# Moving expert additions in the last quarter of the picks from TensorE to VectorE, and moving picks out of one normalisation gap

## The reference

```
ue = jnp.take(u_tab, idx, axis=0)
ve = jnp.take(v_tab, idx, axis=0)
act = jax.nn.gelu(jnp.einsum('thkd,td->thk', ue, t, preferred_element_type=jnp.float32),
                  approximate=False)
return jnp.einsum('thk,thkd->td', (g * act).astype(t.dtype), ve)
```

## Time and profile before

| | us |
|---|---|
| median of 3 runs | 3024.56 (3024.44 to 3024.97) |
| the profiled execution | 3023.42 |
| its span, first to last instruction | 3021.6 |
| TensorE busy | 2738.6 (91%) |
| VectorE busy | 2105.9 (70%) |
| ScalarE busy | 1253.6 (41%) |
| GpSimd busy | 622.1 (21%) |

### The profile page before, as it was taken

The page is one execution under the profiler, slowest core; times in us unless marked ns, Lnnn a source line. Parts: engine busy times, 40 slices in busy tenths (PEclk is TensorE's granted clock), DMA queues, the critical chain, the costliest instruction groups (busy, mean ns, idle before and its releaser), DMA issues. The chain is left out here.

```text
span 3021.6 us, 41715 instructions
## 1 busy us (share of the span) xinstructions
PE 2738.6 (91%) x14564; PEld 2067.9 (68%) x14564; DVE 2105.9 (70%) x4582; ACT 1253.6 (41%) x2946; POOL 622.1 (21%) x531
## 2 busy tenths in 40 slices
PE   6999998889988888798997999599999999999998
PEld 6777788444444444455565777366888989988998
DVE  6895556888878887656687566965546576675887
ACT  3333325444434434555353222354543443333544
POOL 0000000444444444442233233331000000010000
PEclk9999999999999999999998999799999999999999
DMA  6541124999999999999899999995432445543554
GB/s 240 183 168 54 56 91 141 419 420 420 421 417 420 420 419 412 381 418 408 320 399 398 362 417 417 386 376 224 168 133 94 139 149 185 184 149 107 154 184 138
DMA packets 157705, 830.23 MB, mean 275 GB/s; under 512 B 16704, under 2 KB 22080, under 8 KB 91840
## 3 DMA queue, kind: packets, MB, share of 16 engines
q0 software_dynamic: 73728, 536.90, 43.3%
q1 hardware_dynamic: 78240, 271.85, 26.1%
q10 hardware_dynamic: 5536, 18.88, 1.7%
HBM read 825.47 MB, written 2.10 MB: 274 GB/s over the span
## 5 line engine op out<-in xcount | busy, mean ns | idle before, releaser
L750 POOL DMA_INDIRECT slots<-in_experts,consts x295 | 354.2, 1201 | 1036.5 <-DVE consts L2467 521.3
L2492 DVE SCALAR_TENSOR_TENSOR slots<-slots,work 128x1024 f32<-128x1024 f32 x295 | 361.4, 1225 | 93.5 <-DMA slots<-in_experts,consts 81.5
L2091 DVE TENSOR_TENSOR wlo<-w,whi 128x1024 fp32r<-128x1024 f32 x259 | 314.5, 1221 | 70.9 <-ACT whi L1506 70.0
L1078 PE MATMUL psum<-slots,acc 128*128 128x512 f32 x636 | 302.2, 615 | 54.9 <-ACT acc L1724 53.0
L1506 ACT ACTIVATE whi<-w 128x1024 fp32r<-128x1024 f32 x259 | 272.4, 1054 | 138.5 <-PE psum L798 133.4
L750 POOL DMA_INDIRECT split_slots<-in_experts,consts x164 | 200.4, 1222 | 327.6 <-issue 121.6
L1078 PEld LDWEIGHTS psum<-slots,acc 128*128 128x128 f32 x636 | 118.2, 193 | 212.8 <-issue 122.9
L783 PE MATMUL psum<-xres,w 128*128 128x256 f32 x1040 | 240.0, 387 | 0.0
L1712 ACT ACTIVATE consts<-consts 128x1 f32<-128x1 f32 x512 | 100.8, 197 | 333.9 <-DVE slots L2492 190.8
L783 PEld LDWEIGHTS psum<-xres,w 128*128 128x128 f32 x1040 | 198.4, 194 | 46.6 <-issue 20.3
L2492 DVE SCALAR_TENSOR_TENSOR split_slots<-split_slots,work 128x1024 f32<-128x1024 f32 x164 | 200.7, 1224 | 35.8 <-DMA split_slots<-in_experts,consts 29.6
(11 more groups left out here) (367 smaller groups left out, 6030.1 us busy)
## 6 DMA issues: line engine op xcount, KB each, us to landing
w<-in_stream SPq DMA_DIRECT2D x424, 512.0 KB
back_w<-in_back SPq DMA_DIRECT2D x64, 512.0 KB, 3.7
arena<-in_wmod SPq DMA_DIRECT2D x4, 2048.0 KB, 17.2
arena<-in_wmod ACTq DMA_DIRECT2D x8, 1024.0 KB, 5.7
acc<-in_wmod ACTq DMA_DIRECT2D x8, 1024.0 KB, 6.7
slots<-in_experts,consts POOLq DMA_INDIRECT x295
split_slots<-in_experts,consts POOLq DMA_INDIRECT x164
xres<-in_xT SPq DMA_DIRECT2D x1, 2048.0 KB, 9.8
```

The source lines that it names most:

```text
L750: pool.indirect_dma_start(out=slots[slot], out_offset=None, in_=a["experts"], in_offset=bass.IndirectOffsetOnAxis(ap=indices[:, p:p + 1], ...
L1078: mm = pe.matmul(bank(6 + half), diag(p), v[:, half * T:(half + 1) * T], start=(c == 0), stop=(c == PICKS - 1))
L2091: dve.tensor_tensor(wlo[:, s, :, :].rearrange("p k n -> p (k n)"), w32[:, s, :], whi[:, s, :, :].rearrange("p k n -> p (k n)").bitcast(F32 ...
L2492: dve.scalar_tensor_tensor(u, u, 1.0, tokens[:, p // PICKS, :], ALU.mult, ALU.mult, accum_out=inner[:, c:c + 1]).then_inc(sem("dotted"), 1)
```

## The change

Two numbers of the plan are changed. The gap at the end of mlp0 (tile 210) gets the weight 3 and not 8. And `on_dve` also holds from pick 482 on: the picks 482, 483, 486, 487, 490, 491, 494, 495, 498, 499, 502, 503, 506 and 507, seven pairs, are added by VectorE.

```
-    gaps = {SECTIONS["lout0"][0] + 7: 3.5, SECTIONS["pool0"][0] + 1: 3.5, SECTIONS["mlp0"][0] + 63: 8,
+    gaps = {SECTIONS["lout0"][0] + 7: 3.5, SECTIONS["pool0"][0] + 1: 3.5, SECTIONS["mlp0"][0] + 63: 3,
             SECTIONS["xo0"][0] + 7: 3.5, last - 1: LAST_GAP}
...
 def on_dve(p):
 
-    return 336 <= p < 462 and p // 2 % 2 == 1 and p % PICKS < PICKS - 4
+    return (336 <= p < 462 or 482 <= p) and p // 2 % 2 == 1 and p % PICKS < PICKS - 4
```

## The result

The changed kernel is slower: 3039.28 us, median of 5 runs (3035.00 to 3041.82), against 3024.56 us. The ratio is 1.0049, with a 95% interval of 1.0038 to 1.0060. Timed again later, in 12 runs beside 17 of before, it was 3035.34 against 3024.24, ratio 1.0034 (1.0024 to 1.0045). One of these 12 took 6270.86 us, in a slow state; the ratio leaves it out, and the median of the other eleven is 3034.84. Forecast was 3013.4, with a range of 3004 to 3026.

The account below looks back on a forecast made before the run. TensorE was taken to bound the tiles, VectorE the gap behind mlp0, the norm's VectorE-ScalarE chain the smaller gaps. Terms summed to -11.2 us: profiled 3023.42 to 3012.2, median 3013.4, range 3004 to 3026.

Parts of the forecast that it names:

- mlp0: Tiles of mlp0, where TensorE is full: one pair more costs +1.9 us (0.5 to 1.9).
- xq0: Stage behind lout0's gap: no term of its own; the pair that left it was counted in lout0's gap.
- core0: Stage core0: one pair more, between 0 and 1.9 us, half taken, +1.0 us.
- lout0's gap: Gap at lout0's norm: its only pair waits for a late weight and delays the group and scores, +4.1 us.
- xo0: End of xo0: one more pair in the last tile, +0.2; gap without a pair, -8.5; together -8.3 us.
- Rival D: Emptied gap of xo0: whole group at the slow clock, term -4.6 not -8.5; total 3017.3 us; chance 0.12.
- rival B: Transfers set mlp0's pace: terms of xo0, mlp0 and its gap come to nothing; 3031.0 us; chance 0.08.
- The gap of mlp0: Gap behind mlp0, VectorE its chain: six dots and three additions fewer, -11.2 us.
- pool0's gap: Gap at pool0's norm: its pair is weighed later, starts later and delays the group, +5.2 us.
- xo1: Stage xo1: three pairs fewer for TensorE, seven additions more for VectorE, -3.4 us (-5.6 to 0).
- the end: Last picks: one pair fewer, but two additions between VectorE's last dots delay the last one, +3.2 us (0 to 4.5).
- xq1: Rest of xq1: two pairs fewer for TensorE, five additions mostly hidden on VectorE, -3.7 us (-5 to 0).

Follow-up runs that it names:

- the second kernel: The kernel before with only the additions from pick 482 on moved to VectorE, the gap keeping its ten picks: 3022.43 us, ratio 0.9996.
- the eighth: The kernel before with the additions on VectorE from 482 to 503 only, 506 and 507 staying with TensorE: 3017.16 us, ratio 0.9974.
- the second profile: The changed kernel run and profiled once more, nothing altered: median 3035.34 us.

## Why the prediction was wrong

The step that failed most is mlp0's, the overlap of more gathers with full DMA engines, which was put at nothing beside a pair's +1.9; next to it stands xq0, which had no term. By the prediction's own steps:

*core0* (+1.0): the two profiles show +2.3 and +2.4, but kernels with the same plan up to there lie between -1.7 and +2.4. Nothing can be said of it.

*lout0's gap* (+4.1): right in its mechanism to the tenth, 8.45 us of waiting against 8.47, and small by 1.3 to 2.3 us. The term took ScalarE's fourth block from before, 6.7 us behind the column sums; now it comes at 8.5 us (1505.62 to 1514.08), since VectorE scales and adds two rows (0.75 and 1.28 us) ahead of its blocks. From that block to the pair it is 4.17 us, as forecast.

*xq0* (no term): wrong, +3.1. I counted the pairs of the stage and found one fewer. I did not look where in the stage they now stood: the pair that used to follow the second tile follows the first, ahead of the weights that ScalarE makes behind the softmax. In a stage where ScalarE weighs behind something else, a pair costs by its place.

*xo0* (-8.3): the gap itself is right, -7.7 to -7.9 for -8.5. The tiles ahead of it were given 0.2 and cost 2.4, in part since the last residual waits for VectorE, which is at a dot (it starts 1.20 us behind its tile, and 0.03 before), and 5.1 where the clock fell. Rival D, the whole group at the slow clock after the emptied gap, came about for 12 of 32 records: the group takes 8.69 and 1.13 us, with the waits 10.2 from start to end, against 14.2. These slow records cost next to nothing in the changed kernel, since the last four records had to wait 0.39 us for the last block all the same. The Trainium skill's advice against idle gaps (in "TensorE: Matmul & The Clock Gate", "Why this matters for your kernels") was no reason against this edit. The clock was low behind the emptied gap, but it had fallen ahead of it, at about 1624.3 among the norm's sums and products, and it rose 4.9 us into the group. Where a low clock cost time, at the end of xo0, TensorE's waits were of 1.01, 0.32, 0.69 and 1.09 us.

*mlp0* (+1.9): this is the largest mistake, 8.7. It is rival B in part: 6.5 us of it are gone with half the weights' bytes, 2.3 stay, near the forecast. B had a chance of 0.08, and was put aside since VectorE waited only 0.5 us ahead of 42 dots. The sign that the prediction itself gave for B, over 3 us of waits for DMA in mlp0, is there with 12.6. The row says that the gathers were in time, not by how much; the share of 1.02 at 416 GB/s said that nothing could be made up for, and the prediction itself had put the demand at 12.6 us for five more picks. The slack had to be measured, from a transfer's last packet to its dot, and set against that number: it is smallest with 4.5 us at pick 452, and of these some 3 us pass even where a dot waits for nothing else, so that by this estimate 1.5 us were free. And B was priced as all or nothing, so that its time seemed far off; a part of it was enough.

*The gap of mlp0* (-11.2) measured -11.5 and -11.3; *pool0's gap* (+5.2) measured +4.6 and +4.7; *xo1* (-3.4) measured -3.3; *the end* (+3.2) measured +4.0. All right.

*xq1* (-3.7): the additions bring -3.2 in the second kernel and in the eighth, so the term is right. The +3.1 and -0.3 of the changed kernel hold the late signal of the scores besides, for which nothing in the trace of before stood.

Right, within 1 us or little more (2.3 in lout0's gap), was every term on a place that the prediction walked through row by row; wrong were those that it settled by counting (xq0, xo0's tiles) or by a wait that was absent (mlp0). For the second profile the sum closes like this: -11.2 forecast, + 2.3 in lout0's gap, + 3.1 in xq0, + 2.2 in xo0's tiles, + 0.8 over its norm, + 6.7 in mlp0, + 3.4 in xq1, and + 0.1 in all that is left (+1.4 at the start, -1.7 at the very end, +0.3 in the others, rounded) give +7.4. The first profile has 8 us more: 2.8 the clock ahead of xo0, 3.4 in xq1, 3.4 behind L1178, and 1.0 less in lout0's gap.

## What to carry to other kernels

A plan that shares work in proportion moves every stage when one weight is changed: price the places where the work arrives, above all where it lands before a weight or a gather that is made or brought for it later. That nothing waits for a transfer tells nothing of how much later it may come; measure the time from its landing to its use before moving its use ahead, where the DMA engines are full. Taken out of the gap and given to the stages behind it, with the late pairs moved behind the group and the last two additions left to TensorE, the same idea gave 0.4% to 0.5% less time and not 0.3% to 0.5% more.

## What the runs showed of the hardware

The same instruction stream, with the same idle times ahead of it, ran at the lower clock in one execution and at the full one in another (L1360 and the tile behind it, 8.45 us and 5.68 us). An instruction of VectorE that waits for TensorE's product began between 0.04 and 2.3 us after the end of the product's record, and at once behind the semaphore's update wherever the trace holds it: where a releaser is "remote", the end of TensorE's record is not the time of its signal. With half the bytes of its weight tiles, no segment in question of the kernel before changed by more than 1.3 us, though the DMA engines were at 1.02 there: they were full, and not the bound. The share did not tell the two kernels apart either (1.02 at 417 GB/s in both, and 0.99 with half the weights' bytes); the time from a gather's last packet to its dot did, 4.5 us at the least in the one and 2.6 to 3.4 from dot to dot in the other.
